# A decoder layer's expert stage: token rows as the stationary operand, gate-up from four shared pieces of code

## The reference, cut to what matters

```python
logits = t @ router_w + router_b;  top_logit, top_idx = top_k(logits, 4);  gates = softmax(top_logit)
# for each expert e, its tokens' rows:
gu   = t[tok] @ w_gate_up[e] + b_gate_up[e]          # 1024 -> 2048, gate and up in alternate columns
gate = minimum(gu[:, 0::2], 7.0);  up = clip(gu[:, 1::2], -7.0, 7.0)
act  = (up + 1.0) * gate * sigmoid(1.702 * gate)
y    = act @ w_down[e] + b_down[e]                   # 1024 -> 1024
# the four results of a token are summed, weighted by its gates
```

## Time and profile before

| | us |
|---|---|
| median of 3 runs | 3569.02 (3564.10 to 3569.88) |
| profiled execution | 3564.53 |
| its span | 3562.9 |
| PE busy | 3011.3 (85%) |
| DVE busy | 1207.1 (34%) |
| ACT busy | 609.0 (17%) |
| POOL busy | 182.9 (5%) |
| granted TensorE clock, mean | 0.916 |

### The profile page before, as it was taken

How to read it: one execution, slowest core, us unless ns; L and a number is a source line. 1 busy time by engine, 2 the same in 40 slices (tenths; PEclk the granted TensorE clock), 3 DMA queues, 4 the chain that set the end, 5 groups by cost and what they waited for, 6 DMA issues and landing times.

```text
span 3562.9 us, 47319 instructions
## 1 busy us (share of the span) xinstructions
PE 3011.3 (85%) x15924; PEld 2200.9 (62%) x15925; DVE 1207.1 (34%) x3431; ACT 609.0 (17%) x1547; POOL 182.9 (5%) x188
## 2 busy tenths in 40 slices
PE   3477756999997996599999999999999998999990
PEld 1244436666664654487777777777876786777770
DVE  1155440677772563222122222222222221222224
ACT  0011110555551331010000000100110010000100
POOL 0000000000000011000000000000000000000000
PEclk8788875999998995799999999999999999999995
DMA  2512122533003100766544576566876564645835
GB/s 103 192 51 51 39 61 55 151 80 80 13 2 95 54 26 16 263 238 213 175 171 157 201 275 211 199 237 219 280 271 225 203 236 164 241 156 181 290 114 243
DMA packets 306094, 555.15 MB, mean 156 GB/s; under 512 B 80350, under 2 KB 115422, under 8 KB 304840
## 3 DMA queue, kind: packets, MB, share of 16 engines
q1 hardware_dynamic: 265912, 509.39, 42.3%
q0 software_dynamic: 21152, 38.50, 3.1%
q10 hardware_dynamic: 18832, 4.33, 0.6%
HBM read 525.89 MB, written 70.93 MB: 168 GB/s over the span
## 4 chain that ended last, share of the span: by engine, by line
PE 52%; issue 3%; DVE 2%; DVEq 1%; DMA 1%; ACT 1%; ACTq 1%; POOL 0%; POOLq 0%
PE ps L1641 34%; PE ps L1659 16%; PE ps L1664 2%; DVE x L1610 1%; PE ps L1623 1%; ACT xT_e L1527 0%; DMA d_ys<-ys_e,dst 0%; ACTq L1427 0%; DVE gg L1578 0%; DVEq L1427 0%; DVEq L1430 0%; DMA xg<-d_h,src 0%; DVE ys_e L1595 0%; DVEq L1563 0%; ACT ss L1546 0%
## 5 line engine op out<-in xcount | busy, mean ns | idle before, releaser
L1641 PE MATMUL ps<-xT_e,wg 128*128 128x128 f32 (+2 forms) x8192 | 1248.3, 315 | 31.8 <-issue 27.9
L1641 PEld LDWEIGHTS ps<-xT_e,wg 128*128 128x128 f32 x8192 | 1207.6, 197 | 88.2 <-issue 49.1
L1659 PE MATMUL ps<-w_rows,aT 128*128 128x512 f32 x1248 | 567.8, 612 | 11.8 <-issue 10.1
L1659 PEld LDWEIGHTS ps<-w_rows,aT 128*128 128x128 f32 x1248 | 239.2, 195 | 321.3 <-issue 321.3
L1578 DVE TENSOR_SCALAR gg<-ps,bias 128x128 f32<-128x128 f32 (+2 forms) x256 | 101.2, 395 | 703.0 <-PE ps L1641 702.9
L1546 ACT ACTIVATE ss<-gg 128x128 f32<-128x128 f32 (+2 forms) x256 | 88.7, 346 | 888.2 <-DVE gg L1578 887.9
L1546 ACT ACT_TABLE_LOAD x32 | 41.1, 1283 | 881.8 <-issue 881.8
L428 PE MATMUL ps<-w_in,hT_a 128*128 128x430 f32 x512 | 187.4, 528 | 0.1
L724 PE MATMUL ps<-ident_t,sc 128*128 128x128 f32 x880 | 149.6, 286 | 31.0 <-ACT sc L790 27.6
L790 ACT ACTIVATE sc<-sc,nm 128x640 f32<-128x640 f32 (+15 forms) x256 | 161.6, 634 | 67.3 <-DVE nm L832 67.3
L1595 DVE COPY ys_e<-ps 128x1024 f32<-128x1024 f32 x22 | 26.3, 1222 | 423.4 <-PE ps L1664 221.3
(11 more groups left out here) (290 smaller groups left out, 2598.8 us busy)
## 6 DMA issues: line engine op xcount, KB each, us to landing
wg<-in_w_gate_up SPq DMA_DIRECT2D x128, 2048.0 KB, 8.1
w_rows<-in_w_down SPq DMA_DIRECT2D x128, 1024.0 KB, 4.9
wg<-d_ys SPq DMA_DIRECT2D x8, 2048.0 KB, 10.9
d_bias<-d_rev SPq DMA_DIRECT2D x1, 10368.0 KB, 40.5
w_in<-in_w_in SPq DMA_DIRECT2D x1, 6880.0 KB
x_a<-in_x POOLq DMA_DIRECT2D x8, 512.0 KB, 8.5
kn<-d_kn SPq DMA_DIRECT2D x8, 512.0 KB
strip_t<-d_bias SPq DMA_DIRECT2D x8, 512.0 KB
```

The lines of the kernel that those rows point to most:

```text
L1641: mm = pe.matmul(ps[:, j % 2, half * PASS:half * PASS + w], wg[:, j // 2, k, c0:c0 + 255:2], xT[:, k, 0:w], start=(k == 0), stop=(k == KD ...
L1659: mm = pe.matmul(ps[:, 2 + 2 * b + h, :], aT[:, j, b * P:b * P + r], wd[:, c, j % 2, h * 512:(h + 1) * 512], start=(j == 0), stop=(j == JD ...
```

## The change

Gate-up is turned round: the rows (`xT`, as columns) are stationary, and 512 columns of weights move. The result has the rows on the partitions. It is made from four pieces of code, each there once:

| piece | rows | first column of `xT` | units of matmuls | PSUM banks |
|---|---|---|---|---|
| q | 32 | 192 | 1, over 4 chunks at once | 1 |
| g | 64 | 192 | 2, over 2 chunks each | 0, 1 |
| h | 64 | 128 | 2, over 2 chunks each | 0, 1 |
| f | 128 | 0 | 4, one chunk each | 0, 1, 0, 1 |

In a unit, q's four chunks go to four groups of 32 columns of the array and g's and h's two to two groups of 64. A pass uses the pieces of its size, in the order q, g, h, f: 64 rows h; 96 q, h; 128 f; 160 q, f; 192 h, f; 224 q, h, f; 256 g, h, f. The plan has eight numbers a pass, among them a flag each for q, g and h, worked out in three more VectorE steps. Each engine reads the flags and, for a piece that it hasn't got, increments that piece's semaphores itself (`none`).

The activations are computed with 128 partitions x 256 features, in one set of buffers, and then turned on TensorE (`turn_act`) and copied to `aT` by ScalarE (`copy_act`). The biases are no longer transposed at the setup: each pass loads them, broadcast to all partitions (1 MB), between the gate-up and the down weights. The down part of a pass with q or g besides h is a whole block; the last piece is turned in its middle. The down weights lie with two neighbouring rows on a partition (8 KB in one run). The flags, piece lengths and semaphores: `CREDIT` is 16, and the stage has 55 credited semaphores in place of 23.

```diff
@@ stage_setup: the load of b_gate_up and of an identity, 16 transposes and the copy to bgT are gone
@@ stage_plan
+                sp.dma_start(steps[:, :, :], e.c_steps.partition_broadcast(P)).then_inc(s_in, 16)
+                step(dve.tensor_scalar(over[:, 0, :], steps[:, 0, :], r[:, 6:7], None, ALU.is_lt))
+                step(dve.tensor_tensor(steps[:, 1:4, :], steps[:, 1:4, :], bcast(over[:, 0:1, :], [P, 3, 7]), ALU.mult))
+                step(dve.tensor_reduce(r[:, 7:10], steps[:, 1:4, :], AX.X, ALU.add))
@@ stage_experts
+        SEG = {"q": (P // 4, 192, 1), "g": (P // 2, 192, 2), "h": (P // 2, 128, 2), "f": (P, 0, 4)}
+        BANK = {"q": (1,), "g": (0, 1), "h": (0, 1), "f": (0, 1, 0, 1)}
@@ sync, a chunk of wg
-                            sp.wait_ge(s_gu, CREDIT + JD * i + 2 * (c + 1) - JD)
+                            sp.wait_ge(s_gu["h"], CREDIT + 2 * i + c // 2 + 1 - 2)
+                            sp.wait_ge(s_gu["f"], CREDIT + 4 * i + c + 1 - 4)
+                        sp.dma_start(bias[:, :], e.b_gate_up[0][one, :].rearrange("o n -> (o n)").partition_broadcast(P)).then_inc(s_bias, 16)
@@ scalar: sigmoid(k, j) for q, g, h; then for f each sigmoid followed by the copy of the piece before
+                            with act.If(hasq > 0):
+                                copy_act(i, "q", 0)
+                            with act.If(hash_ > 0):
+                                copy_act(i, "h", 0)
+                            next_rows(i + 1, after)
+                            with act.If(n > 3 * P // 4):
+                                copy_act(i, "f", 3)
+                            with act.If(hash_ > 0):
+                                copy_act(i, "h", 1)
@@ vector
+                            dve.wait_ge(s_gu[k], CREDIT + per * i + j + 1)
+                            for g in range(groups):
+                                read = dve.tensor_tensor(gu[part, :], ps[part, BANK[k][j], :], bias[part, cols], ALU.add)
+                            read.then_inc(s_rd[k], 1)
+                            dve.tensor_scalar(gg[:, :], gu[:, 0::2], LIMIT, None, ALU.min).then_inc(s_g[k], 1)
+                            dve.tensor_scalar(uu[:, :], gu[:, 1::2], LIMIT, -LIMIT, ALU.min, ALU.max).then_inc(s_u[k], 1)
+                            dve.scalar_tensor_tensor(vv[:, :], uu[:, :], 1.0, gg[:, :], ALU.add, ALU.mult).then_inc(s_v[k], 1)
+                            dve.wait_ge(s_sig[k], CREDIT + per * i + j + 1)
+                            dve.tensor_tensor(aa[:, AA[k][j], :], vv[:, :], ss[:, :], ALU.mult).then_inc(s_a[k], 1)
+                            dve.wait_ge(s_a[k], CREDIT + per * i + j + 1)
+                        def none(k):
+                            for s in (s_rd[k], s_a[k], s_g[k], s_u[k], s_v[k]):
+                                dve.sem_inc(s, SEG[k][2])
+                        with dve.If(hasq > 0):
+                            piece("q")
+                        with dve.Else():
+                            none("q")
...
@@ tensor
+                            for kk in range(KD):
+                                for g in range(groups):
+                                    mm = pe.matmul(ps[g * kind:(g + 1) * kind, BANK[k][j], :], xT[:, kk, t0:t0 + kind], wg[:, j * groups + g, kk, :],
+                                                   start=(kk == 0), stop=(kk == KD - 1))
+                        with pe.If(hasq > 0):
+                            unit("q", 0)
+                        with pe.Else():
+                            none("q")
...
+                        with pe.If(hash_ > 0):
+                            pe.wait_ge(s_rd["g"], CREDIT + 2 * i + 1)
+                            unit("h", 0)
+                            pe.wait_ge(s_rd["g"], CREDIT + 2 * i + 2)
+                            pe.wait_ge(s_rd["q"], CREDIT + i + 1)
+                            unit("h", 1)
+                        with pe.If(n > 3 * P // 4):
+                            for j in range(4):
+                                if j == 0:
+                                    pe.wait_ge(s_rd["h"], CREDIT + 2 * i + 1)
...
+                                unit("f", j)
+                                if j:
+                                    pe.wait_ge(s_a["f"], CREDIT + 4 * i + j)
+                                    turn_act("f", j - 1)
...
+                        pe.wait_ge(s_aTc["f"], CREDIT + 4 * i + 2)
+                            turn_rows(i + 1, 2, CREDIT + 4 * i + 3)
+                        def last_turn(k, j):
+                            pe.wait_ge(s_a[k], CREDIT + SEG[k][2] * i + SEG[k][2])
+                            pe.wait_ge(s_xTc, CREDIT + 4 * i + 4 + 3)
+                            turn_act(k, j)
+                            pe.wait_ge(s_aTc[k], CREDIT + SEG[k][2] * i + SEG[k][2])
```

More of the change, by code:

```diff
@@ L42 @@
 CAP = S
-CREDIT = 8
+CREDIT = 16
 def give_credit(eng, sems):
@@ L1419, in stage_experts @@
         s_wd = [sem(f"e_wd{c}") for c in range(NCH)]
-        s_gu, s_g, s_up, s_sig, s_a, s_down, s_y, s_sd, s_dch = (sem("e_" + n) for n in
-            ("gate_up", "gate", "up", "sigmoid", "act", "down", "y", "scatter_done", "dve_chain"))
+        s_bias = sem("e_bias")
+        s_gu, s_rd, s_g, s_u, s_v, s_sig, s_a, s_aT, s_aTc = ({k: sem(f"e_{n}_{k}") for k in "qghf"} for n in
+            ("gate_up", "gate_up_read", "gate", "up", "product", "sigmoid", "act", "actT", "actT_copied"))
+        s_down = [sem(f"e_down{b}") for b in range(2)]
@@ L1448, in by_blocks, with flags @@
[L1448 to L1456 removed]
+                by_rows(eng, n, body, sizes[:half])
+        def flags(eng, i):
+            return [flag(eng, i, f) for f in range(3)]
         with nc.Block() as block:
@@ L1666, in down @@
-                                mm.then_inc(s_down, 1)
-                        by_blocks(pe, n, down)
+                                if c == 2:
+                                    last_turn(*turn)
+                                for h in range(2):
+                                    for j in (2 * c, 2 * c + 1):
+                                        mm = pe.matmul(ps[:, 2 + 2 * b + h, :], aT[:, j, b * P:(b + 1) * P], wd[:, c, j % 2, h * 512:(h + 1) * 512],
+                                                       start=(j == 0), stop=(j == JD - 1))
@@ new lines, in whole, with half @@
+                                mm.then_inc(s_down[b], 1)
+                        def half(t0, turn):
+                            r = P // 2
+                            for c in range(NCH):
+                                pe.wait_ge(s_wd[c], CREDIT + 16 * i + 16)
+                                if c == 2 and turn:
+                                    last_turn(*turn)
+                                for j in (2 * c, 2 * c + 1):
+                                    for h in range(2):
+                                        mm = pe.matmul(ps[h * r:(h + 1) * r, 4, :], aT[:, j, t0:t0 + r], wd[:, c, j % 2, h * 512:(h + 1) * 512],
+                                                       start=(j == 0), stop=(j == JD - 1))
+                                mm.then_inc(s_down[1], 1)
@@ new lines, in _ @@
+                        with pe.If(n > 3 * P // 4):
+                            whole(0, ("f", 3))
+                        with pe.Else():
+                            pe.sem_inc(s_down[0], NCH)
+                        with pe.If(hash_ > 0):
+                            with pe.If(hasq + hasg > 0):
+                                whole(1, ("h", 1))
+                            with pe.Else():
+                                half(128, ("h", 1))
+                        with pe.Else():
+                            with pe.If(hasq > 0):
+                                half(192, None)
+                            with pe.Else():
+                                pe.sem_inc(s_down[1], NCH)
```

328 lines of the change are left out of this document (200 added, 128 removed).

## The result

| | before | after |
|---|---|---|
| median, us | 3566.56 (3560.66 to 3569.88, 4 runs) | 3789.68 (3787.49 to 3797.66, 4 runs) |
| span of the profiled execution | 3562.9 | 3787.0 |
| granted TensorE clock, mean | 0.916 | 0.87 |
| PE busy | 3011.3 | 2937.2 |
| ACT busy | 609.0 | 763.3 |

The ratio is 1.0632, with a 95% interval from 1.0609 to 1.0654: 6.3% slower. I had forecast 3675, 3.0% slower. The sign, and nearly every place where time goes or comes from, were forecast; the amount is over twice the forecast.

The account below looks back on a forecast made before the run. TensorE was taken to bound the kernel, with 52% of the chain. Terms from -234 (gate-up matmuls) to +134 (wait after q) summed to +109 on 3564.5 us; forecast 3675 us, 3.0% slower, 8-in-10 range 3570 to 3790.

Parts of the forecast that it names:

- Matmul time: TensorE's gate-up and down matmuls: gate-up falls from 1238 to 1004 us (-234), down from 606 to 577 (-29).
- The last piece's turn in the down part: TensorE turns the last piece and waits for its copy, 42 times 1.35 us: +57 us.
- Stalls for code: TensorE's stalls for loading code where arms change fall from 101 to 25 us: -76 us.
- The wait after q: TensorE waits for VectorE's late report of skipped g in 20 passes, 6.5 or 7.2 us each: +134 us.
- The wait at the start: In 11 passes beginning with h or f, TensorE waits 5.0 or 5.7 us for skipped-piece reports: +59 us.
- Clock: TensorE at half clock after 31 gaps, 2.1 us each (65), plus some 15 before down: +80 us.
- the looser part before down: Share of the clock term for the stretch between gate-up and down: some 15 us.
- Turn phase: Between gate-up and down, transposes wait behind ScalarE's copies: 177 us in all against 88 before, +89 us.
- the reports pass early: Rival: VectorE's sequencer sends skipped pieces' increments before TensorE asks; 59 + 134 + 65 us go, 3417 us; 18%.
- q gets its quadruple: Denied by a rival: q's matmuls run only in pairs, not four at once; 108 us more, 3783 us; 10%.
- hardly any code is loaded: Denied by a rival: each skipped piece is a jump that still loads code; +100 us, 3775 us; 10%.

Follow-up runs that it names:

- e2: Changed kernel with VectorE counting the skipped pieces right after reading its flags, ahead of its first piece: 3596.68 us, ratio 1.0103.
- e5: Changed kernel with a dummy sigmoid ahead of ScalarE's loop and VectorE's counts of skipped pieces made one pass ahead: 3430.27 us, ratio 0.9634.
- e8: e5 with TensorE's gate-up code no longer shared, each of the seven arms having its own copy of its pieces: 3679.40 us, ratio 1.0312.
- e7: Changed kernel with 7 matmuls of unused output put on TensorE after the 32-row piece, to fill the wait: 3753.49 us, ratio 1.0541.
- e1: Changed kernel with one dummy sigmoid on ScalarE ahead of its loop: 3660.88 us, ratio 1.0279.
- e10: Changed kernel with VectorE again loading the expert's number at the top of its loop, empty passes included: 3816.08 us, ratio 1.0698.
- e12: e5 with VectorE loading the next pass's count only inside the passes that are run, not in the empty ones: 3420.53 us, ratio 0.9599.
- e11: e1 with a Copy in place of the Sigmoid ahead of ScalarE's loop: 3798.41 us (2 runs), ratio 1.0650.
- e4: Changed kernel with the 32-row piece taken out, steps of 64 rows: 3802.48 us, ratio 1.0676.
- e9: e5 with the 32-row piece taken out, steps of 64 rows: 3550.85 us, ratio 0.9962.
- b1: Kernel before with the dummy sigmoid put ahead of ScalarE's loop: 3558.73 us, ratio 0.9990.

## Where the prediction held and where it failed

It forecast +109 us; the spans differ by +224. It had the dearest item right, TensorE's waits for counts of pieces that a pass hasn't got (e2: 188 us). What it lacked is in the turn phase. Term by term:

- *Matmul time*, -234 and -29: right. q's 7.07 us fit the four at once that I had taken. In e5, where little disturbs the stretches, gate-up is 1036.8 us against 1004 + 20 for f's transposes, with some 15 of the clock's 45 in it.
- *The last piece's turn in the down part*, +57: too large. TensorE has this wait 42 times, as forecast, but for 0.7 us (0.9 in six of them) and not 1.35: 31 us. So it was luck that e5's down, 636.8, fits 577 + 57: some 21 us of it are the clock's.
- *Stalls for code*, -76: the direction is right, the size too large. TensorE's "issue" waits in the loop were 68 us before and are 22 after, 46 less, and a part of those may only lie hidden behind the waits for counts: e5, without them, has 55. The code itself went: 113 packets in the loop before, 4 after. e8 shows that the sharing of the code matters (241 us). The waits before (us in total, times, longest) were:

```profile
PE ps L1623 <- issue: 30.4, 15, 3.6
PE ps L1641 <- issue: 27.9, 16, 7.6
PE ps L1659 <- issue: 10.1, 12, 6.0
```

- *The wait after q*, +134: 148.8 us in the trace. In the pass shown the chain is the one that I had built: eviction, scatter, ScalarE's register loads, table load, sigmoid, product, branch; h starts 13.9 us into the pass, forecast 13.4. e2 took the wait away.
- *The wait at the start*, +59: +46, and 8 more in the first pass, where the counts stood behind the wait for the bias; I had no term for that.
- *Clock*, +80: +130, the second term that was too small. That the clock falls behind a gap was right (e7), a gap's price too: 2.2 us after q, forecast 2.1. So were the 65 us for 31 gaps: gate-up's share of the loss grew by 63. Wrong were the 15 us for the looser part before down: the turn phase and the down matmuls behind it lost 69 us more than before, and e1 took 65 of them away.
- *Turn phase*, +89: **this is the step that failed.** It was +143 by the table, whose 122.5 us before hold 30 of "issue" waits that I had booked under code; against the 88 that I had started from, 265.2 is 177 more, twice the term. e1 puts 94 us of that to the loads (265.2 to 171.1; I had forecast 177 in all). The step made the clock's term too small as well. I worked its times out from the sigmoid (1.7 us after the matmuls) and copies of 0.38, each 0.3 later than the one before; the trace has a table load of 1.28 ahead of the copies. The row was there: the earlier trace rows has a load in the pass ahead of its first sigmoid, with the loop's only other activation a copy. I priced that load in q's chain and did not ask why there was one in every pass, and so put the loads ahead of the copies at nothing.
- *After the last matmul*, no term: -12. VectorE's loop lost a register load that the 15 empty passes ran (e10, e12).

What the failed step was worth: without the loads the change measures 1.0279, which on the median of 3566.56 is 3666 us, where I had forecast 3675. That they lie so close is in part luck: the stalls for code brought some 30 us less than forecast and the wait after q cost 15 more, while the turn in the down part cost 26 less and the end of the kernel came 12 earlier. Against the rivals: *the reports pass early* was wrong, the counts wait in VectorE's order as forecast; q gets its quadruple; hardly any code is loaded in the loop any more.

That the loads cost what e1 gave back is shown. Why they are there is an inference. The *ScalarE: Activation LUTs* page of the Trainium skill (section on table sets) says that cheap functions such as copy are in every set. By that a copy never needs a load, and once the sigmoid's set was there (e1) the copies did without. But 75 of the 138 loads stand directly ahead of copies. What fits all three kernels (e1, e11 and the changed one): the loads are put in when the program is built, from what is known of the set at that place; where ways meet that come with different sets, nothing is known, and the next activation of each arm gets a load, of whatever kind it is. By this reading the set left before the loop was another one; so the first arm was in doubt, and each arm that can be skipped passed the doubt on. That this is how loads are placed is not shown.

## What to carry to other kernels

Where an engine skips work and has to account for it, let it count the skipped pieces first, or a pass ahead: behind its real work the counts cost 188 us here, and together with the other waits they hid all that the smallest piece was worth (nothing in e4, 117 us in e9). Look at ScalarE's table loads when branches are added around activations: one sigmoid of one column ahead of the loop was worth 126 us, and nothing in the kernel before, whose loads lay beside TensorE's work (b1). And when a wait on TensorE is priced, price the clock behind it in every stretch that gets looser, the down matmuls after a loose turn phase included.

## What the hardware showed that I had not expected

- An ACT_TABLE_LOAD takes 1.283 us whatever stands behind it, and comes ahead of copies too: three times in the 6 us of the turn phase shown, each with its copy 0.02 us behind it.
- In a stretch that is only loose, not idle (10.5 us with 4.8 of TensorE's work, its two longest gaps 2.0 and 3.1 us), the clock fell as after a full stop, to 0.63 on the mean, and the matmuls after it took 10.07 us for 7.13.
- With seven arms of gate-up code (e8) TensorE stood 28 times ahead of gate-up with no releaser in the profile, 7.5 us on the mean and up to 16.5, and the clock fell behind these stands as behind other waits: its price rose from 45 to 106 us. The kernel before loaded as much code in its loop (113 packets of 16 KB, e8 107) and stood for a third of that.
- In six passes the scatter of results took 3 to 6 us to land in the changed kernel and 7 to 9 in e1, with the DMA share at 1.00 to 1.04 for 0.41 to 0.83, and TensorE, at the end of that chain, waited up to 11.4 us after q.
- Register loads count where nothing covers them: an empty pass of VectorE takes 2.22 us with two `value_load`s (e5), 1.36 (the changed kernel) to 1.50 (e12) with one.
